# Down projection of a hybrid decoder step: row factors of the second pass spread by small DMAs, and a last half tile cut 384 + 128 instead of 256 + 256

## The reference

```
h   = rmsnorm(x, g_pre_mix);  p = h @ w_in                    # 6 blocks of 1024 columns
mix = w_o( sigmoid(gate_conv) * short_conv_branch + sigmoid(gate_pool) * pooling_branch )
x   = x + rmsnorm(mix, g_post_mix)
f   = relu(rmsnorm(x, g_pre_mlp) @ w_up)^2 @ w_down           # 1024 -> 4096 -> 1024
x   = x + rmsnorm(f, g_post_mlp)
rmsnorm(x, g) = x * rsqrt(mean(x*x) + 1e-6) * g
```

## Time and profile before

| | |
|---|---|
| median of 3 runs | 998.44 us (997.85 to 999.02) |
| the profiled execution's own time | 997.95 us |
| its span, slowest core | 996.9 us (all cores 996.4 to 996.9) |
| PE busy | 979.6 us, 98% of the span |
| DVE, ACT, POOL busy | 473.5, 323.2, 230.1 us |
| granted TensorE clock | 0.999 to 1.000 on every core |

### The profile page before, as it was taken

The page is one execution under the profiler, slowest core; times in us unless marked ns, Lnnn a source line. Parts: engine busy times, 40 slices in busy tenths (PEclk is TensorE's granted clock), DMA queues, the critical chain, the costliest instruction groups (busy, mean ns, idle before and its releaser), DMA issues.

```text
span 996.9 us, 16428 instructions; the slowest of 8 cores (996.4 to 996.9 us)
## 1 busy us (share of the span) xinstructions
PE 979.6 (98%) x5463; PEld 484.9 (49%) x5463; DVE 473.5 (47%) x858; ACT 323.2 (32%) x639; POOL 230.1 (23%) x362
## 2 busy tenths in 40 slices
PE   7999999999999999999999999999999999999997
PEld 6544444444444444444445545555445555544444
DVE  4667855334634331251667886533365444301413
ACT  4422232227633333201333224222584333301111
POOL 7111211115421132032113242111362111120110
PEclk9999999999999999999999999999999999999999
DMA  9999999991782239489856366964209422231342
GB/s 216 177 179 143 123 135 129 115 155 29 117 130 82 74 95 234 148 211 146 201 80 78 54 83 86 258 91 65 37 8 127 89 66 73 74 117 43 94 118 85
DMA packets 46690, 113.76 MB, mean 114 GB/s; under 512 B 7056, under 2 KB 9360, under 8 KB 46352
## 3 DMA queue, kind: packets, MB, share of 16 engines
q0 software_dynamic: 40272, 91.51, 55.5%
q1 hardware_dynamic: 6048, 20.91, 6.7%
q10 hardware_dynamic: 288, 0.30, 0.1%
HBM read 164.20 MB, written 18.49 MB: 183 GB/s over the span
## 4 chain that ended last, share of the span: by engine, by line
PE 94%; issue 1%; DMA 1%; DVE 1%; ACT 1%; POOL 1%; DVEq 0%; ACTq 0%; POOLq 0%
PE PS L135 93%; DMA WS<-w_in 1%; ACT TM L152 1%; PE PS L139 1%; DVE AR L155 1%; POOL AR L155 0%; DVE TM L165 0%; ACT AR L152 0%; POOL AR L126 0%; ACT STAT L152 0%; DVE AR L165 0%; DVE STAT L442 0%; POOL WS L126 0%; DVEq L220 0%; DVE TM L155 0%
## 5 line engine op out<-in xcount | busy, mean ns | idle before, releaser
L135 PE MATMUL PS<-AR,WS 128*128 128x512 bf16 (+1 forms) x3664 | 656.6, 340 | 2.9 <-DVE STAT L442 1.6
L135 PEld LDWEIGHTS PS<-AR,WS 128*128 128x128 bf16 x3664 | 321.1, 98 | 328.8 <-issue 4.8
L135 PE MATMUL PS<-WS,AR 128*128 128x512 bf16 (+1 forms) x1392 | 296.2, 374 | 0.0
L152 ACT ACTIVATE TM<-PS 128x512 f32<-128x512 f32 (+3 forms) x252 | 140.3, 570 | 351.3 <-PE PS L135 349.4
L135 PEld LDWEIGHTS PS<-WS,AR 128*128 128x128 bf16 x1392 | 135.8, 98 | 154.3
L155 DVE TENSOR_TENSOR AR<-TM 128x512 bf16<-128x512 f32 (+1 forms) x200 | 120.1, 615 | 137.7 <-ACT TM L152 133.2
L126 POOL DMA_DIRECT2D WS<-wd_bf x96 | 51.8, 540 | 267.9 <-PE PS L135 261.3
L152 ACT ACTIVATE TM<-PS,CS 128x512 f32<-128x512 f32 (+1 forms) x80 | 49.6, 623 | 131.5 <-PE PS L135 123.5
L126 POOL DMA_DIRECT2D WS<-w_in x96 | 52.6, 556 | 165.3 <-PE PS L135 164.7
L442 DVE RECIPROCAL STAT<-STAT 128x1 f32<-128x1 f32 (+1 forms) x54 | 8.7, 162 | 135.2 <-ACT STAT L152 135.0
L155 DVE TENSOR_TENSOR TM<-PS,TM 128x512 f32<-128x512 f32 (+1 forms) x40 | 24.4, 610 | 95.3 <-PE PS L135 94.4
(11 more groups left out here) (62 smaller groups left out, 337.2 us busy)
## 6 DMA issues: line engine op xcount, KB each, us to landing
WS<-w_in POOLq DMA_DIRECT2D x96, 256.0 KB, 8.9
WS<-wd_bf POOLq DMA_DIRECT2D x96, 256.0 KB, 3.2
WS<-w_up POOLq DMA_DIRECT2D x64, 256.0 KB, 7.3
wd_bf<-w_dn POOLq DMA_DIRECT2D x8, 1024.0 KB, 37.2
y_p<-AR SPq DMA_DIRECT2D x15, 512.0 KB, 5.0
AR<-x_p SPq DMA_DIRECT2D x9, 512.0 KB, 15.2
WS<-w_oc POOLq DMA_DIRECT2D x16, 256.0 KB, 16.0
WS<-w_o POOLq DMA_DIRECT2D x16, 256.0 KB, 26.2
```

The source lines that it names most:

```text
L135: return self.add("pe", lambda e: e.matmul(out, lhsT, rhs, start=start, stop=stop), reads=[lhsT, rhs], writes=[out], signal=sig, name="mm")
L152: return self.add("act", lambda e: e.activation(out, in_, func, **kw), reads=rd, writes=wr, name=name)
```

## The change

A row of HBM per tile takes the place of the matmul. After `rstd`, `st_sq(i)` writes the 128 factors (128 partitions x 1 f32) to row i of a new HBM tensor `r_dr` (`rout`, SP), and for tiles 0 to 7 `st_row(i)` at once reads that row back into all 128 partitions (`rrow`, SP, waits for `rout`) in a new view `RB` of SBUF, the ninth tile of `x1`, which the first pass does not use. Tile 8's row is read at unit 38, since it takes the place of tile 0's. `st_scale` has no matmul and takes no bank; its `hsc` operations read `RB`. In `last_tile` the pieces become 384 and 128 columns; the order of the operations after each piece is unchanged.

```diff
+    r_dr = nc.dram_tensor("r_dr", [NTILE_B, 128], F32, kind="Internal").ap()
...
+        RB = _view(AR, A_X1 + 8 * 4096, F32, [D])
...
                 def st_sq(i):
-                    nx_r[i] = mean_sq(JNK5, XQ[i % 2])
-                    rstd(nx_r[i][1])
+                    _, ss = mean_sq(JNK5, XQ[i % 2])
+                    rstd(ss)
+                    w = P.dma("sp", r_dr[i].rearrange("(p a) -> p a", a=1), ss, "rw%d" % i, name="rout")
+                    nx_r[i] = w
+                    if i < 8:
+                        st_row(i)
+
+                def st_row(i):
+                    P.dma("sp", RB[:, i % 8 * 128:(i % 8 + 1) * 128], bass.AP(r_dr.tensor, i * 128, [[0, 128], [1, 128]]),
+                          "rr%d" % i, name="rrow", deps=[nx_r[i]])
 
                 def st_scale(tiles):
-                    b = banks.one()
                     n = len(tiles) * 128
                     a = tiles[0] * 128
-                    for c, i in enumerate(tiles):
-                        P.mm(PS[:, b, c * 128:(c + 1) * 128],
-                             bass.AP(STT_, nx_r[i][0], [[64, 128], [0, 128]]), IDF[:, :], start=True, stop=True)
+                    r0 = tiles[0] % 8 * 128
                     for k in range(KC):
-                        P.stt("dve", hT[:, k, a:a + n], hT[:, k, a:a + n], cs(C_GPM + k), PS[:, b, 0:n],
+                        P.stt("dve", hT[:, k, a:a + n], hT[:, k, a:a + n], cs(C_GPM + k), RB[:, r0:r0 + n],
                               ALU.mult, ALU.mult, name="hsc")
-                    banks.give(b)
...
                 at(37, st_scale, (4, 5, 6, 7))
+                at(38, st_row, 8)
                 at(43, st_scale, (8,))
...
-                        for h in range(2):
-                            pm = PS[:, b[h], 0:256]
+                        for h, (o, n) in enumerate(((0, 384), (384, 128))):
+                            pm = PS[:, b[h], 0:n]
...
-                                         w[:, kk, h * 256:(h + 1) * 256], start=(q == 0 and kk == 0),
+                                         w[:, kk, o:o + n], start=(q == 0 and kk == 0),
...
-                            op, sh = square(pm, 256)
                             if h == 0:
+                                op, sh = square(pm, n)
                                 P.tt("dve", ss, ss, sh, ALU.add, name="ssa")
+                                times_g(y1[:, 0:n], pm, a1, op)
                             else:
+                                op, sh = square(pm, n)
                                 P.act(sh, sh, AF.Sqrt, bias=ss, name="sqrt")
-                            times_g(y1[:, h * 256:(h + 1) * 256], pm, a1 + h * 256, op)
+                                times_g(y1[:, o:o + n], pm, a1 + o, op)
```

## The result

| | before | after |
|---|---|---|
| median | 998.7 us | 1126.0 us |
| ratio of the means | | 1.1278, interval 1.125 to 1.1306 |
| profiled execution, its span | 997.95, 996.9 us | 1123.93, 1122.8 us |
| PE busy | 979.6 us | 983.6 us |
| clock by core | 0.999 to 1.000 | 0.944 to 0.949 |

The forecast was 996.3 us, with a range up to 998.6. In some runs, of the kernel before too, the cores of one die show a lower clock and take longer; the times (medians) and ratios here leave such runs out, which for the kernel that reads the rows late leaves one run of four.

What follows compares the result with a forecast made beforehand. PE was taken to bound the kernel, busy 979.6 of 996.9 us. Removed matmuls (2.00 us) and the shorter last square (0.10), all else priced 0, took 2.1 us off the 998.44 median: 996.3 us, range 995.3 to 998.6.

Steps and rivals of the forecast that it cites:

- Part 1: Second pass's input preparation: removing eighteen f32 records, two per matmul, at 0.111 us each saves 2.00 us of PE.
- Part 2: What replaces the f32 matmuls: eighteen DMAs on the SP queue, `hsc` reading SBUF, another bank order; all priced 0.
- Price 0, under cover of those 9 us: Down projection, unit 48: later loads delay `post1` banks, slack falls from 22 us to 9, so PE loses nothing.
- rival (c): SP's loads and row writes outlast their cover: 17 us of PE idle at unit 48, about 1013 us; chance 0.10.
- The steps of the chain: SP queue, second pass's input: load, small write, next load; forecast 9.0 + 1.5 us each, later 5.0 + 1.5.
- The point of decision: PE idles if the last square runs later than about 441 us, some 1.3 us more per small write.
- rival (b): After 480 us, PE waits for a weight or x transfer and hands the gain back: 997.2 to 998.6 us; chance 0.13.
- The bank order: Second pass: without `st_scale`'s takes banks rotate differently; `w_o` still starts with pair 0/1, price 0, 0.1 us at most.
- `hsc` from SBUF: Second pass on DVE: factor row read from SBUF instead of PSUM, 1.2 us more at most under idle time, price 0.
- Part 3: Last tile in 384 and 128 columns: no change on PE (7.02 against 7.04 us), shorter last square gains 0.10 us.

Runs made afterwards that it cites:

- second probe: Kernel before plus SP-queue writes in the second pass: one of 4-byte pieces 4096 bytes apart behind the x loads, then six kinds twice; profiled time 1000.2 us.

## Why the prediction was wrong

**Part 1 held.** The f32 matmuls are worth about what was said: 2.00 us worked out; 1.2 us by the runs without DMAs, 2.1 by the median span over all cores in the version with the transpose (994.75 against 996.8), last tile included.

**Part 2 failed at one term: the landing of `rout`.** I took 7.1 us for the first, from the earlier trace rows, and 1.5 beyond the load's landing for the others, and called 8.0 the far end. The runs showed 22.3 us for the first and 23.6 in the median, and steps of 19.5 to 28 us where I had 10.5 and 6.5. With it "Price 0, under cover of those 9 us" fell. The rows chosen had 128 rows too, but of 64 bytes each (8 KB); 128 pieces of 4 bytes into 512 bytes are another thing, as 14.7 against 1.5 us in the second round of the second probe shows. The trace of before had no write in pieces this small, and I bounded the unseen from above by a transfer of 512 KB, as if bytes were the only cost. That was no bound. The fixed cost of about 2.0 us that the prediction cites changed nothing in this. The Trainium skill, "DMA: Bandwidth & Descriptors", section "Anatomy of one DMA", gives it there for DMAs issued from GpSimd; `rout` goes out on SP.

**The mechanism of rival (c) was right and its price was not.** The last square came at 547.09 instead of 431.3 (c: 457), the first `post1` square at 548.53 (c: 458), and PE stood 71.3 us at unit 48 (c: 17):

```profile
547.09 1.06 ACT L152 ACTIVATE TM<-TM 128x1024 bf16<-128x1024 f32 x1 [15.80 <-DMA TM<-x_s]
...
548.53 0.58 ACT L152 ACTIVATE TM<-PS 128x512 bf16<-128x512 f32 x1
```

The steps of the chain were 19.5 to 28 us against 17.0 and 10.2. The point of decision was right: with the pieces 4096 bytes apart the last square of the slowest core ran at 442.12, and PE waited 1.3 us for a bank at 451; I had put that point at 441. But even there the forecast's steps of 10.5 and 6.5 us were short; the loads went at 377.9, 390.5, 405.6, 413.5, 420.0, 427.1 and 435.0, up to 9 us later than I had them. So on that core even harmless writes used up the 9 us of slack; six of the eight cores show no such wait.

**A cost without a place in the working: the writes hold up transfers of other queues.** I priced 2304 extra packets as extra traffic, in rival (b), with nothing specific for it. The run with late rows shows 59.8 to 98.3 us for weight loads of 256 KB and PE waiting 32.4 to 60.5 us for them, although no load waits there for a write to land. I had not worked out how much lead the weights have at all. Rival (c) had neither this nor the clock, and its 1013 us stood 113 us short.

**"Small" was read as "cheap".** The Trainium skill, "DMA: Bandwidth & Descriptors", section "Specifications", says that below 512 bytes a transfer does a read-modify-write. I did not weigh it. The runs agree that side-by-side small pieces are dear, but not that size alone decides: 4-byte pieces 64 bytes apart land in 6.4 us and leave the kernel's time where it was (ratio 1.0009), and 128 pieces of 64 bytes took 1.5 us in the median. No run shows a read-modify-write itself.

**The bank order and `hsc` from SBUF held**: eight `hsc` took 5.39 us against 5.36, and without the DMAs no new wait appeared. **Part 3 held** in the trace, 7.04 us again, and 0.11 less after the last square, too little to be timed. The 81 ns per matmul of 128 columns of the Trainium skill ("TensorE: Matmul & The Clock Gate", "Back-to-back issue gap") stay refuted: the last tile's 7.04 us has no room for 0.78 more.

## What to carry to other kernels

A column of single values written to HBM as a contiguous row is not a small transfer: it goes out as many small pieces that land close together. Turn the data on an engine first (pieces of 64 and 128 bytes did no harm here), or spread the pieces. A DMA that holds up no other issue can still stop the program if it occupies the engines that bring the weights: price it by pieces and where they land, not by bytes, and against the lead of the most urgent transfer beside it. When a run's cores differ, look at each core's clock before a time is explained by waits. And before an upper bound is called one, ask whether the row it comes from shares the form of the access, not only the size.

## What was not expected of the hardware

One DMA of 512 bytes in 128 side-by-side pieces takes 7.2 us with hardly anything else under way, 7.4 to 16.1 us beside one 256 KB load per 3.9 us, and 18.5 to 26 us in the loaded stretch, during which the DMA engines show shares of 0.98 to 1.23 at 14 to 33 GB/s. With the pieces 64 bytes apart the same DMA lands in 6.4 us in the loaded stretch. While nine of the side-by-side writes run, weight loads that took 15.7 to 18.6 us take 43.0 to 51.5. That pieces wait for each other where they share bytes is a guess: it fits the large differences, but not the second probe, where 512 bytes between the pieces helped further than 64 (2.4 against 6.8 us), and no run shows it inside an engine.
